# Head 3 of the GLA stage: fill packed into 18 slots, two early output projections moved between its last pairs, and the casts around them reordered

## The reference, cut to what matters

```
proj = h @ w_in ; q, k, v, r = split(proj)            # 4 heads, dk 128, dv 256
gate_pre = (h @ w_gate_a) @ w_gate_b + b_gate
logf = log_sigmoid(gate_pre) / 16
# per head, chunks of 64 frames:
b = cumsum(logf)
inter = (q * exp(b)) @ s0                             # state s0: dk x dv
attn[l, m] = sum_k q[l,k] k[m,k] exp(b[l,k] - b[m,k]) # m <= l
o = inter + attn @ v
s_new = exp(b_last) * s0 + (k * exp(b_last - b))^T @ v
# then
o = o * rsqrt(mean(o*o) + eps) * g_onorm * silu(r)
out = o @ w_out                                       # 1024 x 1024
x = x + rms_norm(out, g)
```

## Time and profile before

| | |
|---|---|
| median of 3 runs | 2674.08 us (2668.62 to 2683.92) |
| profiled execution, its own time | 2674.08 us |
| its span, first to last instruction | 2672.2 us |
| PE busy | 2545.0 us, 95% |
| DVE, ACT, POOL busy | 971.8, 822.3, 447.3 us |
| mean granted clock of PE | 0.978 of 2.4 GHz |
| L158 POOL w_lo, mean of 180 | 2.481 us |
| L151 ACT w_hi cast, mean of 180 | 1.047 us |
| GLA stage | about 0 to 540 us |

### The profile page before, as it was taken

How to read it: one execution, slowest core, us unless ns; L and a number is a source line. 1 busy time by engine, 2 the same in 40 slices (tenths; PEclk the granted TensorE clock), 3 DMA queues, 4 the chain that set the end, 5 groups by cost and what they waited for, 6 DMA issues and landing times.

```text
span 2672.2 us, 41797 instructions
## 1 busy us (share of the span) xinstructions
PE 2545.0 (95%) x17566; PEld 2384.9 (89%) x17566; DVE 971.8 (36%) x1913; ACT 822.3 (31%) x1618; POOL 447.3 (17%) x186
## 2 busy tenths in 40 slices
PE   6999999998999999999998999999899999999997
PEld 5878887798999999999997777688899999999996
DVE  5445444517322222222248344425522222222227
ACT  4445444535221121121134444435411211211221
POOL 1101020111221221221211101012112112211210
PEclk9999999999999999999998999899999999999998
DMA  3101011014111111111114100003211111111113
GB/s 106 40 9 48 23 39 38 21 52 138 63 40 47 45 41 47 39 47 39 59 36 141 53 25 17 29 24 99 95 48 40 47 39 47 40 46 47 39 60 123
DMA packets 63089, 139.06 MB, mean 52 GB/s; under 512 B 8688, under 2 KB 39920, under 8 KB 62960
## 3 DMA queue, kind: packets, MB, share of 16 engines
q1 hardware_dynamic: 33984, 103.60, 12.1%
q10 hardware_dynamic: 28976, 33.64, 4.1%
HBM read 117.81 MB, written 19.40 MB: 51 GB/s over the span
## 4 chain that ended last, share of the span: by engine, by line
PE 78%; DVE 5%; issue 2%; ACT 2%; ACTq 0%; DMA 0%; DVEq 0%
PE banks L201 51%; PE banks L181 18%; PE banks L1746 1%; DVE norm_acc L463 1%; DVE h_lo L548 1%; DVE norm_acc_x L477 1%; DVE y L524 1%; PE banks L1250 1%; PE banks L1246 1%; PE banks L1266 1%; PE banks L1234 1%; PE banks L1251 1%; PE banks L1274 1%; PE banks L323 0%; PE banks L1900 0%
## 5 line engine op out<-in xcount | busy, mean ns | idle before, releaser
L158 POOL TENSOR_TENSOR w_lo<-w_raw,w_hi 128x1024 fp32r<-128x1024 f32 x180 | 446.0, 2481 | 2152.6 <-ACT w_hi L151 2152.6
L181 PE MATMUL banks<-h_hi,w_hi 128*128 128x384 f32 (+1 forms) x1224 | 432.4, 353 | 5.6 <-ACT gla_v_tok L1996 3.1
L181 PE MATMUL banks<-h_lo,w_hi 128*128 128x384 f32 (+1 forms) x1224 | 410.8, 336 | 0.0
L181 PE MATMUL banks<-h_hi,w_lo 128*128 128x384 f32 (+1 forms) x1224 | 410.4, 335 | 0.0
L151 ACT CAST w_hi<-w_raw 128x1024 fp32r<-128x1024 f32 x180 | 187.0, 1047 | 463.7 <-DMA w_raw<-in_units 462.8
L201 PE MATMUL banks<-h_hi,w_hi 128*128 128x384 f32 (+1 forms) x1368 | 301.8, 329 | 0.0
L201 PE MATMUL banks<-h_lo,w_hi 128*128 128x384 f32 (+1 forms) x1368 | 301.3, 328 | 0.0
L201 PE MATMUL banks<-h_hi,w_lo 128*128 128x384 f32 (+1 forms) x1368 | 301.3, 328 | 0.0
L201 PE MATMUL banks<-mlp_a_hi,w_hi 128*128 128x384 f32 (+1 forms) x1344 | 296.6, 329 | 1.5 <-issue 1.3
L201 PE MATMUL banks<-mlp_a_lo,w_hi 128*128 128x384 f32 (+1 forms) x1344 | 295.1, 327 | 0.0
L201 PE MATMUL banks<-mlp_a_hi,w_lo 128*128 128x384 f32 (+1 forms) x1344 | 295.0, 327 | 0.0
(11 more groups left out here) (193 smaller groups left out, 3145.3 us busy)
## 6 DMA issues: line engine op xcount, KB each, us to landing
w_raw<-in_units SPq DMA_DIRECT2D x180, 512.0 KB, 3.5
x_scratch<-y ACTq DMA_DIRECT2D x48, 192.0 KB, 2.5
norm_x<-x_scratch ACTq DMA_DIRECT2D x48, 192.0 KB, 3.3
x_scratch<-y ACTq DMA_DIRECT2D x24, 160.0 KB, 1.8
norm_x<-x_scratch ACTq DMA_DIRECT2D x24, 160.0 KB, 3.1
y<-in_x SPq DMA_DIRECT2D x16, 192.0 KB, 4.8
norm_x<-in_x ACTq DMA_DIRECT2D x16, 192.0 KB, 3.3
out_y<-y SPq DMA_DIRECT2D x16, 192.0 KB, 2.8
```

The costliest lines, as they stand in the source:

```text
L158: c.nc.gpsimd.tensor_tensor(c.w_lo[:, s], c.w_raw[:, s], c.w_hi[:, s].bitcast(F32), ALU.subtract).then_inc(self.ready, 1)
L181: mm = chip.nc.tensor.matmul(out, w, x, start=(first and n == 0), stop=(last and n == 2))
```

## The change

Six edits, all in the class `Gla`:

1. `STEPS[3]` goes from 21 to 18: the jobs of head 3 end in slot 17, the last of pair 5, and no longer in slot 20.
2. `HIGHS[3]`: the casts of units 23 to 27 move from slots 8, 13, 15, 18 and 24 to 6, 11, 13, 16 and 21.
3. `FILL_AT`: two of the four early projections run in slots 23 (behind output of pair 7) and 25 (between update and output of pair 8); the other two stay behind pair 8.
4. ACT: silu(3) and early_high(0) move from pair 7, ahead of its output copy, to the end of pair 6; early_high(1) from pair 8 to the end of pair 7.
5. DVE: early_low(0) and (1) go to the ends of pairs 6 and 7; early_low(2) stands where early_low(1) stood, ahead of the gated products.
6. ACT, before the first pair of head 0: the cast of unit 4 goes from before level_exp(0) to behind level_exp(1), and copy_value(8) ahead of the cast of unit 5.

```diff
--- before.py
+++ after.py
@@ -1569,10 +1569,11 @@
     SCAN = 9 * CHUNK
     EARLY = 2 * (GH - 1)
     LEAD = 3 * KT * BMAX
-    STEPS = (PARTS * NPAIR, PARTS * NPAIR, PARTS * NPAIR, 21)
+    STEPS = (PARTS * NPAIR, PARTS * NPAIR, PARTS * NPAIR, 18)
     GATE_AT = (1, 3, 3)
     HIGHS = ({2: 6, 4: 7, 10: 8, 15: 9}, {4: 4, 6: 5, 10: 6, 13: 7, 16: 8, 19: 9}, {4: 4, 6: 5, 10: 6, 13: 7, 16: 8, 19: 9},
-             {4: 4, 8: 5, 13: 6, 15: 7, 18: 8, 24: 9})
+             {4: 4, 6: 5, 11: 6, 13: 7, 16: 8, 21: 9})
+    FILL_AT = (23, 25)
 
     def __init__(self, chip, name, before, after, ins):
         self.chip, self.before, self.after, self.ins = chip, before, after, ins
@@ -1821,6 +1822,8 @@
         def fill(h, slot):
             for job, k in self.plan[h][slot]:
                 job_step(job, k)
+            if h == GH - 1 and slot in self.FILL_AT:
+                end_early(self.FILL_AT.index(slot))
 
         def end_early(m):
 
@@ -1934,7 +1937,7 @@
                 output(h, p)
                 fill(h, self.PARTS * p + 2)
 
-        for m in range(JOB_BANKS):
+        for m in range(len(self.FILL_AT), JOB_BANKS):
             end_early(m)
         for i in range(2 * NB):
             if i == 0:
@@ -2164,12 +2167,12 @@
         take_start(2, 1)
         take_start(2, 2)
         chunk_decays(0)
-        ws.high(act, 4)
         level_exp(0)
         copy_value(7)
         level_exp(1)
+        ws.high(act, 4)
+        copy_value(8)
         ws.high(act, 5)
-        copy_value(8)
         take_jobs(0, -1)
 
         for h in range(GH):
@@ -2186,11 +2189,6 @@
                 else:
                     take_jobs(h, slot)
                     level_exp(g + 2)
-                if h == GH - 1 and p == 7:
-                    silu(h)
-                    early_high(0)
-                if h == GH - 1 and p == 8:
-                    early_high(1)
                 if slot in self.HIGHS[h]:
                     ws.high(act, self.unit(h, self.HIGHS[h][slot]))
                 if h < GH - 1 and p == self.GATE_AT[h] + 1:
@@ -2213,6 +2211,11 @@
                     load_gain(h)
                 if h < GH - 2 and p == 6:
                     load_gate(h + 2)
+                if h == GH - 1 and p == 6:
+                    silu(h)
+                    early_high(0)
+                if h == GH - 1 and p == 7:
+                    early_high(1)
         output_root(GH)
         for j in range(NB):
             scale_outputs(GH, j)
@@ -2423,18 +2426,16 @@
                     gate_flat(h + 1)
                 if h < GH - 1 and p == self.GATE_AT[h] + 1:
                     gate_sums(h + 1)
-                if h == GH - 1 and p == 7:
-                    early_low(0)
+                if h == GH - 1 and p in (6, 7):
+                    early_low(p - 6)
         output_variance(GH)
         output_inverse(GH)
-        early_low(1)
+        early_low(2)
         for j in range(NB):
             gated(GH - 1, 2 * j)
             gated(GH - 1, 2 * j + 1)
             if j:
                 low_parts(j - 1)
-            if j == 1:
-                early_low(2)
         low_parts(NB - 1)
         self.vector_end_wave(dve)
```

## The result

The changed kernel takes 2696.83 us (median of 6 runs, 2696.21 to 2697.73) against 2674.68 (2668.62 to 2683.92): ratio 1.0083, 95% interval 1.0070 to 1.0095, so 22 us slower. The forecast was 2688.5, range 2675 to 2698.

A forecast was written before the change was run, and what follows sets the result against it. PE was taken as the bound, running matmuls nearly back to back, so the start of its dense tail decides. Mark +9.1, behind it -0.9, clock 2.5 + 1.0, start +2.8: +14.5 on 2674.08, said as 2688.5 us, range 2675 to 2698.

The forecast's parts named there:

- the mark: First matmul of blocks 6 and 7 of the output projection, at 530.31 before; predicted 9.1 us later, at 539.4.
- Packing: Head 3's fill in 18 slots: pair 3 starts at 459.8 instead of 462.00, pair 6 at 491.9 against 490.71.
- Pair 6 without fill: Head 3: pair 6's own chain shows and takes 8.0 us; pair 7's scores at 499.9 against 500.19.
- Pair 7's chain: Serial waits on ACT and DVE from pair 7's scores: early projection 0 at 11.8 us, pair 8's scores at 18.0.
- Behind pair 8's scores: Cast, update, early projection 1, output, old tail and early_low(2), from 18.0 to the mark at 39.5 us after pair 7's scores.
- third chance of the slow level: Early projection 1, with pair 8's small gaps: a third chance of the slow level at 3 us, counted as 1.0.
- early_low(2): On DVE, now ahead of the gated products before the mark: delays them by 2.13 us.
- The start: Head 0: w_lo of unit 4 ready at 104.6, +2.2, and slot -1's matmuls slow for longer, +0.6; in all +2.8 us.
- Behind the mark: After the mark: PE's 0.9 us wait for the bank copy goes, a slow clock stretch costs 2.5.
- rival 4: Before head 0's first scores: DVE's first decay 1.5 us shorter, scores sooner, start term -1.5 instead of +2.8; 2684.3, 2 in 100.
- Rival 3: PE at 1.2 GHz from pair 7 through early projections 1 to 3 and behind the mark; 2694 to 2700, 12 in 100.
- later waits of PE are relative to it, so I let it stay: Heads 0 to 2: the start's +2.8 us shift carries through unchanged, heads 1 and 2 adding nothing.

The follow-up runs named there:

- e5: Changed kernel with silu, early casts, early subtractions and unit 27's cast back in their old places, one early projection left in pair 8; 2683.38 us, ratio 1.0024.
- e3: Changed kernel with the cast of weight unit 27 back in slot 24, behind pair 7's output copy; 2692.32 us, ratio 1.0059.
- e2: Changed kernel without edit 6, the start of head 0 put back; 2688.13 us, ratio 1.0050.
- e7: Changed kernel with early_low(2) back between the gated products of blocks 1 and 2; 2690.66 us, ratio 1.0053.
- e1: Kernel before with edit 6 alone, the reordered start of head 0; 2681.32 us, ratio 1.0024.
- e4: Kernel before with head 3's fill packed into 18 slots and the casts of units 23 to 26 earlier; 2681.16 us, ratio 1.0015.
- e8: Kernel before with head 3's fill front-loaded in slots 0 to 8, pair 6 keeping its fill; 2672.71 us, ratio 0.9991.
- e6_delay1: Kernel before with one extra ACT copy behind chunk_decays(0), ahead of level_exp(0); 2677.06 us, ratio 0.9998.
- e10: Kernel before with head 3's fill front-loaded and value copies 7 and 8 ahead of the first level_exp; 2677.67 us, ratio 1.0004.
- e9: Kernel before with value copies 7 and 8 on ACT ahead of the first level_exp; 2678.01 us, ratio 1.0001.
- e6_delay2: Kernel before with two extra ACT copies behind chunk_decays(0); 2681.53 us, ratio 1.0004.

## Why the prediction was right, and where it was short

The direction and the range held; the point was 8.3 us too low, and the time lies at the upper end of the range, outside the 2682 to 2696 that the forecast had as its own. The excess over the forecast in the profile is 9.1 us: 6.1 from the steps in heads 1 and 2, 2.5 between head 3's start and the mark, 0.6 behind it, less 0.1 at the start. By its own steps:

- **Packing**: right. Pair 3 2.2 us sooner and pair 6 0.95 later from head 3's start (predicted 2.2 and 1.2).
- **Pair 6 without fill**: right, 8.9 us instead of 8.0 (500.41 to 509.32); the last 0.9 because PE's output already ran at the slow level (1.12 and 1.22 us a pair of matmuls, 0.65 and 0.70 at full level before).
- **Pair 7's chain**: right almost to the step: early_low(0) 5.3 after pair 7's scores (5.3), early projection 0 at 12.0 (11.8), unit 27's cast at 16.5 (16.3), pair 8's scores at 18.3 (18.0). PE idles 5.8 us between pair 7's scores and its output, not "over 8" as the signs had it. e5 shows the edits of the tail as the cause, e3 the part of unit 27 (2.3 us).
- **Behind pair 8's scores**: 24.1 us to the mark instead of 21.5. I had given early projection 1 a third chance of the slow level; it did run at it (529.75 to the output at 536.77). In e2, which has the same order here, it ran at the 2.4 GHz level, and the mark came 21.3 us behind pair 8's scores, the predicted value. So the chain was right and the clock term is 0 or about 3; the 1.0 was an average over the two, and which came was luck.
- **early_low(2)**: 2.1 predicted; e7's profile gives 3.6, with the clock of the turns in it.
- **The start**: wait 5.29 instead of 3.06, +2.2 as predicted, fill at 104.39 (104.6), head 1 at +2.7 with the clock (2.8). In time e1 costs 3.5 to 9.1 us, more than the 2.7; part of this stays open.
- **Behind the mark**: the wait of 0.9 is gone, and PE is at the slow level up to about 557, so both terms are there. Their size can't be told: the rest runs from 2139.9 to 2148.0 over the profiles of the table, so that the +2.2 of this pair, near the predicted 1.6, may be chance.
- **The two rules**: DVE's first decay took 0.96 once w_lo was away (2.51 before), as the Trainium skill (SBUF — State Buffer, SBUF: two separate sides) has it, and it was worth nothing, since the scores waited for the fill; rival 4 falls. Silu followed its table load without a drain (load at 509.23, cast at 512.45), so the rule of the Trainium skill (ScalarE: Activation LUTs, What ACT_TABLE_LOAD costs) would have put the chain 1.4 too high.

```profile
99.09 0.96 DVE L2350 TENSOR_TENSOR gla_qd<-gla_e,y 128x768 f32<-128x768 f32 x1 [0.53 <-ACT gla_e L2116]
```

- **Rival 3** named the time that came (2694 to 2700) but not its way: PE was slow in early projection 1 and at the mark, not in projections 2 and 3 (6.5 us for 36 matmuls), and most of what the forecast lacks lies in heads 1 and 2. Its own sum was also put too high: 9.1 - 0.9 + 2.8 with a clock term of 8 to 11 gives 2693 to 2696.
- **The step that failed** is "later waits of PE are relative to it, so I let it stay": I took heads 1 and 2 to be as in the one profile of before. They hold a wait in pair 2 behind which PE falls to 1.2 GHz in some executions, 3.05 us each. In the profile pair compared here these are 6.1 of 23.6 us, a term that the prediction put at nothing. The changed kernel showed both in its profile, the kernel before neither. That the total stayed in the range in spite of it is owed to the range's width and not to the working.

What stays open: how the start of head 0 acts on the steps. The changed kernel's executions lie close together (2693.53 to 2700.59 over 15 of them; 2696.21 to 2697.73 for the six in the comparison), and so do those of e1 (2679.60 to 2684.12) and e5 (2681.54 to 2686.05), which share edit 6, while those of before spread over 13 to 18 us on each chip. All seven profiles whose first scores came over 0.6 us late had both steps, and those of before, e2, e4, e8 and e6_delay1, within 0.3 us, had 0, 0, 2, 0 and 1; e10, 1.2 sooner, had both, and e9, 4.0 sooner, half a one (1.49 us in head 2). e5 and e6_delay2 also lost 1.5 us in pair 4 of head 0. This would fit a shift that makes steps likelier, and so would the groups of executions above; e4 and e10 speak against a shift alone.

## What to carry to other kernels

Work put into a gap of one engine is paid in the queues of the engines that prepare it: here 5.3 us on ACT and 2.6 on DVE went ahead of the recurrence's own steps, and PE's waits from pair 7's scores to pair 8's grew from 3.0 us (1.36 and 1.66) to 7.9 (3.28, 2.54 and 2.11). Before moving an instruction ahead, list what stands behind it on its own engine and who waits for that; and ask by which event a buffer's reload is released, since a cast moved ahead of that event only moves the wait. A term of a few us next to PE's clock needs several executions of both kernels, not one profile of each, and where executions fall into two groups, look at how many lie in each before comparing medians.

## What the runs showed of the hardware

The same 12 matmuls behind the same 1.8 us wait took 2.19 us in one execution and 3.98 in another (e9, e10), and two stretches of heads 1 and 2, with a wait of 0.91 us in each, were granted 1.00 in one execution and 0.80 and 0.81 in another of the same instructions (before, e4). Which short gaps cost a stretch at 1.2 GHz, about 3 us each here, is thus not fixed by the instructions up to there. Executions of the unchanged kernel on one chip fell into two groups some 7 us apart (medians of 16 and 15 executions, 2674.5 and 2681.5), the upper at a lower mean granted clock.
